# One-core two-block network in fp32 halves: the shifted norm ahead of the first FFN is shared out over three engines, and the later stages' tiles begin at other offsets

## What is computed

```python
x = x + gt1 * ((g_att * y_att + g_rwkv * y_rwkv) @ w_o[l])
h = rms_norm(x, norm2_w[l]) * (1.0 + sc2) + sh2
x = x + gt2 * conv_ffn(h, w_up[l], conv_w[l], conv_b[l], w_down[l])
```

## Time and profile before

| | |
|---|---|
| median of 3 runs | 2418.88 us (2418.67 to 2420.12) |
| the profiled execution: time, span | 2418.01 us, 2416.7 us |
| PE busy | 2328.0 us of the span |
| DVE, ACT, POOL busy | 1434.3, 691.2, 884.0 us |
| mean granted TensorE clock | 0.986 of full speed |

### The profile page before, as it was taken

One profiled execution on the slowest core, in us unless ns is written; L12 is line 12 of the kernel. 1 busy time (PEld: TensorE's weight loads), 2 busy tenths in 40 slices (PEclk: granted clock), 3 DMA queues, 4 the chain that ended last, 5 costly groups with the idle time before them and its releaser, 6 DMA issues.

```text
span 2416.7 us, 33857 instructions
## 1 busy us (share of the span) xinstructions
PE 2328.0 (96%) x14384; PEld 1836.3 (76%) x14384; DVE 1434.3 (59%) x1782; ACT 691.2 (29%) x864; POOL 884.0 (37%) x418
## 2 busy tenths in 40 slices
PE   6999999799999999799999999999999999999998
PEld 4776776577776787588888777888878888888887
DVE  5222323678877513767675588788843467888633
ACT  3122122443443423222222233322222333222212
POOL 4313221111111344444444444444444434444442
PEclk8999999899999999899999999999999999999999
DMA  6433332212122243233333223333332323333331
GB/s 238 133 105 102 113 94 77 57 47 52 46 48 48 64 143 93 60 101 100 97 112 89 79 83 104 96 96 96 103 105 84 102 79 87 96 97 99 114 91 54
DMA packets 412038, 222.56 MB, mean 92 GB/s; under 512 B 33823, under 2 KB 409458, under 8 KB 410610
## 3 DMA queue, kind: packets, MB, share of 16 engines
q1 hardware_dynamic: 383074, 206.14, 29.5%
q10 hardware_dynamic: 28816, 14.27, 2.2%
HBM read 214.61 MB, written 5.77 MB: 91 GB/s over the span
## 4 chain that ended last, share of the span: by engine, by line
PE 89%; DVE 6%; DMA 2%; ACT 1%; issue 1%; POOL 1%; SPq 1%; ACTq 0%; DVEq 0%; POOLq 0%
PE bank L312 88%; PE bank L315 1%; SPq L1514 0%; DMA rw_sixteen<-inverses 0%; DMA inverses<-rw_solved 0%; DVE h_low L2096 0%; DMA w_raw<-in_w_att_out 0%; DVE g_c L2302 0%; POOL w_low L308 0%; DVE sq L664 0%; DVE rw_keep L1480 0%; DVE sq L660 0%; DVE rw_terms L1566 0%; DMA vec_rows<-in_c 0%; DVE sq L566 0%
## 5 line engine op out<-in xcount | busy, mean ns | idle before, releaser
L308 POOL TENSOR_TENSOR w_low<-w_raw,w_high 128x1024 fp32r<-128x1024 f32 (+1 forms) x331 | 849.4, 2568 | 1462.2 <-ACT w_high L301 1462.2
L312 PE MATMUL bank<-h_high,w_high 128*128 128x512 f32 x2008 | 809.2, 403 | 25.8 <-DVE h_low L671 9.6
L312 PE MATMUL bank<-h_low,w_high 128*128 128x512 f32 x2008 | 787.5, 392 | 0.0
L301 ACT CAST w_high<-w_raw 128x1024 fp32r<-128x1024 f32 (+1 forms) x331 | 358.6, 1085 | 885.7 <-PE bank L312 863.5
L312 PE MATMUL bank<-h_high,w_low 128*128 128x512 f32 x2008 | 510.2, 393 | 0.0
L312 PEld LDWEIGHTS bank<-h_high,w_high 128*128 128x128 f32 x2008 | 379.1, 189 | 132.2 <-issue 27.1
L312 PEld LDWEIGHTS bank<-h_high,w_low 128*128 128x128 f32 x2008 | 376.0, 188 | 84.4 <-issue 5.3
L312 PEld LDWEIGHTS bank<-h_low,w_high 128*128 128x128 f32 x2008 | 379.9, 189 | 78.7 <-issue 4.1
L312 PE MATMUL bank<-g_high,w_high 128*128 128x512 f32 x352 | 139.1, 395 | 2.3 <-ACT g_c L2281 2.3
L312 PE MATMUL bank<-g_low,w_high 128*128 128x512 f32 x352 | 138.9, 395 | 0.0
L2174 DVE TENSOR_TENSOR x_res<-bank,x_res 128x512 f32<-128x512 f32 x32 | 22.1, 689 | 168.4 <-PE bank L312 168.3
(11 more groups left out here) (375 smaller groups left out, 2820.4 us busy)
## 6 DMA issues: line engine op xcount, KB each, us to landing
w_raw<-in_w_in SPq DMA_DIRECT2D x54, 512.0 KB, 4.9
w_raw<-in_w_up SPq DMA_DIRECT2D x44, 512.0 KB, 3.8
w_raw<-in_w_ffn_gate SPq DMA_DIRECT2D x44, 512.0 KB, 3.8
w_raw<-in_w_ffn_up SPq DMA_DIRECT2D x44, 512.0 KB, 3.9
w_raw<-in_w_ffn_down SPq DMA_DIRECT2D x32, 704.0 KB, 4.5
w_raw<-in_w_ada SPq DMA_DIRECT2D x32, 512.0 KB, 3.8
w_raw<-in_w_in ACTq DMA_DIRECT2D x25, 512.0 KB, 4.1
w_raw<-in_w_down SPq DMA_DIRECT2D x16, 704.0 KB, 4.5
```

Source lines behind the costliest of these rows:

```text
L301: self.A.copy(self.w_high[:, u % SPLIT_SLOTS, 0:k * P], self.raw_of(key)[:, 0:k * P]).then_inc(*self.S.rounded(*key))
L308: self.G.tensor_tensor(self.w_low[:, slot, 0:k * P], self.raw_of(key)[:, 0:k * P], self.w_high[:, slot, 0:k * P].bitcast(F32), ALU.subtrac ...
L312: return self.T.matmul(out, lhsT, rhs, start=start, stop=stop, skip_group_check=True)
```

## The change

It has two parts.

**The shifted norm** (`shifted_norm` in place of `norm`, `h_dve`, `h_act`, `h_pool`). The last square is no longer added by DVE: PE accumulates ones x rinv (the first seven squares), and then ones x sq (the eighth). The second unit of the FFN, ("f", 0, 1), is rounded by ACT and lowered by POOL ahead of the root. The engines then share the tiles. Even tiles: DVE makes sq = x * gain * rinv, ACT adds the shift while rounding into h_high, and DVE makes h_low = (sq + shift) - h_high. Odd tiles: POOL makes rooted = x * rinv, ACT makes h_high = rooted * gain + shift, then less = h_high - shift, and DVE makes h_low = rooted * gain - less. PE (`first_pair_pe`) runs four matmuls for each tile, two units at once, and both low passes behind them.

**The placement.** A tile of 32 bytes (`shift_less`) and one of 96 bytes (`lead`) come ahead of the large tiles, and one of 64 bytes (`lead_shared`) within the scope of the mixers. Nothing reads the last two. Start addresses, bytes over a multiple of 256:

| tiles | before | after |
|---|---|---|
| x_res, h_high, h_low, w_raw, w_high, w_low, rinv, sq | 128 | 128 |
| f_high, f_low, f_c, and the same of g0 and g1 | 0 | 128 |
| ev_high, ev_low, od_high, od_low | 0 | 128 |
| mg_a, mg_r (high and low), mg_both, att, mixed | 192 | 128 |
| the RWKV tiles rw_ar to rw_reach | 192 | 128 |
| ident, ones, head_ones | 160 | 192 |

```diff
--- before.py
+++ after.py
@@ -647,42 +647,6 @@
         for k in range(DT):
             V.scalar_tensor_tensor(src[:, k, :], src[:, k, :], gain(k), self.rinv[:], ALU.mult,
                                    ALU.mult).then_inc(*S_.dve_norm(name, "scaled", k))
-
-    def h_dve(self, name, src, gain, shift=None):
...
-    def h_low_of(self, queue, name, k):
...
-    def h_pool(self, name):
...
-    def h_act(self, name, shift=False):
...
-    def h_ready(self, name):
-        return lambda k: [(self.S.h_low_odd if k % 2 else self.S.h_low_even).at(name, k)]
@@ -2187,7 +2151,10 @@
                 V.wait_ge(*self.own("dve"))
                 V.tensor_scalar(x, x, first(n), None, ALU.mult).then_inc(*S_.dve_norm())
                 V.wait_ge(*self.own("dve"))
-            self.add_square(self.rinv, x, name, "squares", n)
+            if name == "wo" and n == DT - 1:
+                V.tensor_tensor(square, x, x, ALU.mult).then_inc(*S_.dve_norm(name, "squares", n))
+            else:
+                self.add_square(self.rinv, x, name, "squares", n)
             if gain and not to:
                 V.tensor_scalar(x, x, gain(n), None, ALU.mult).then_inc(*S_.residual("gained", n))
             if to and not first:
@@ -2222,14 +2189,64 @@
-    def norm(self, name, before, gain, shift=None):
-
-        self.sum_pe(name, self.S.dve_norm.at(before, "squares", DT - 1))
-        self.sum_dve(name)
-        self.root_act(name)
-        self.h_dve(name, self.x, gain, shift)
-        self.h_act(name, shift is not None)
-        self.h_pool(name)
+    def shifted_norm(self, before):
+        T, A, V, G, S_ = self.T, self.A, self.V, self.G, self.S
+        rooted, less = self.f_c[:, 0, 0, :], self.f_c[:, 1, 0, :]
+        gain, shift = self.gain2, lambda k: self.mod[:, 3 * DT + k:3 * DT + k + 1]
+        T.wait_ge(*S_.dve_norm.at(before, "squares", DT - 2))
+        self.empty(7)
+        self.mm(self.bank[7][:], self.ones[:], self.rinv[:], True, False)
+        T.wait_ge(*S_.dve_norm.at(before, "squares", DT - 1))
+        self.mm(self.bank[7][:], self.ones[:], self.sq[:, 0, :], False, True).then_inc(*S_.norm_sum("ffn"))
+        self.round_unit(("f", 0, 1))
+        self.root_act("ffn")
+        for k in range(DT):
+            if k % 2:
+                A.wait_ge(*S_.h_low_odd.at("ffn", k))
+                A.activation(self.h_high[:, k, :], rooted, ACT.Identity, bias=shift(k),
+                             scale=gain[:, k:k + 1]).then_inc(*S_.act_norm("ffn", "high", k))
+                if k > 2:
+                    A.wait_ge(*S_.h_low_even.at("ffn", k - 2))
+                A.wait_ge(*self.own("act"))
+                A.activation(less, self.h_high[:, k, :].bitcast(F32), ACT.Identity,
+                             bias=self.shift_less[:, k:k + 1]).then_inc(*S_.act_norm("ffn", "less", k))
+            else:
+                A.wait_ge(*S_.dve_norm.at("ffn", "normed", k))
+                A.activation(self.h_high[:, k, :], self.sq[:, k // 2 % 2, :], ACT.Identity,
+                             bias=shift(k)).then_inc(*S_.act_norm("ffn", "high", k))
+        V.tensor_scalar(self.shift_less[:], self.mod[:, 3 * DT:4 * DT], -1.0, None, ALU.mult).then_inc(*S_.dve_norm("ffn", "less"))
+        self.sum_dve("ffn")
+        V.wait_ge(*S_.act_norm.at("ffn", "root"))
+        def normed(k):
+            V.wait_ge(*self.own("dve"))
+            V.scalar_tensor_tensor(self.sq[:, k // 2 % 2, :], self.x[:, k, :], gain[:, k:k + 1], self.rinv[:], ALU.mult,
+                                   ALU.mult).then_inc(*S_.dve_norm("ffn", "normed", k))
+        normed(0)
+        for k in range(DT):
+            if k % 2 == 0 and k + 2 < DT:
+                normed(k + 2)
+            if k % 2:
+                V.wait_ge(*S_.act_norm.at("ffn", "less", k))
+                V.scalar_tensor_tensor(self.h_low[:, k, :], rooted, gain[:, k:k + 1], less, ALU.mult,
+                                       ALU.subtract).then_inc(*S_.h_low_even("ffn", k))
+            else:
+                V.wait_ge(*S_.act_norm.at("ffn", "high", k))
+                V.scalar_tensor_tensor(self.h_low[:, k, :], self.sq[:, k // 2 % 2, :], shift(k),
+                                       self.h_high[:, k, :].bitcast(F32), ALU.add, ALU.subtract).then_inc(*S_.h_low_even("ffn", k))
+        self.lower_unit(("f", 0, 1))
+        G.wait_ge(*S_.act_norm.at("ffn", "root"))
+        for k in range(1, DT, 2):
+            if k > 2:
+                G.wait_ge(*S_.h_low_even.at("ffn", k - 2))
+            G.tensor_tensor(rooted, self.x[:, k, :], self.rinv[:], ALU.mult).then_inc(*S_.h_low_odd("ffn", k))
@@ -2239,20 +2256,24 @@
             self.f_high = self.sb(f"{name}_high", [P, FT, S], F32R, ctx)
             self.f_low = self.sb(f"{name}_low", [P, FT, S], F32R, ctx)
             self.f_c = self.sb(f"{name}_c", [P, 2, 2, S], F32, ctx)
+            if not before:
+                self.shifted_norm("wo")
             self.ffn_pe(name, norm, both, before)
             self.ffn_act(name, norm, biases, before)
             if before:
                 self.ffn_ahead_dve(name, norm, taps)
             else:
                 self.ffn_dve(name, taps, biases, both)
-            self.ffn_pool(name)
+            self.ffn_pool(name, before)
             self.project(f"{name}_down", name, FT, scale, following, self.f_high, self.f_low,
                          lambda k: [self.S.parts.at(name, k)], **to)
     def ffn_pe(self, name, norm, both, before):
-        ready = self.ahead(norm) if before else self.h_ready(norm)
+        ready = self.ahead(norm) if before else None
+        if not before:
+            self.first_pair_pe(name, norm)
         for n in range(FT):
-            for j in range(2):
+            for j in range(2) if n or before else ():
                 b = 2 * (n % 2) + j
                 self.empty(b)
                 self.product((name, n, j), self.bank[b][:], *self.h_parts(), ready=ready)
@@ -2262,6 +2283,27 @@
                 ready = None
         self.end("pe", name)
+    def first_pair_pe(self, name, norm):
+        T, S_ = self.T, self.S
+        keys = [(name, 0, 0), (name, 0, 1)]
+        slots = [self.number[key] % SPLIT_SLOTS for key in keys]
+        tile = lambda t, j, k: t[:, slots[j], k * P:(k + 1) * P]
+        for j, key in enumerate(keys):
+            T.wait_ge(*S_.rounded.at(*key))
+            self.empty(j)
+        for k in range(DT):
+            T.wait_ge(*S_.h_low_even.at(norm, k))
+            for j in range(2):
+                self.mm(self.bank[j][:], tile(self.w_high, j, k), self.h_high[:, k, :], k == 0, False)
+                self.mm(self.bank[j][:], tile(self.w_high, j, k), self.h_low[:, k, :], False, False)
+        for j, key in enumerate(keys):
+            T.wait_ge(*S_.lowered.at(*key))
+            for k in range(DT):
+                ins = self.mm(self.bank[j][:], tile(self.w_low, j, k), self.h_high[:, k, :], False, k == DT - 1)
+            ins.then_inc(*S_.product(*key))
+            self.emptied[j] = (S_.conv, key)
     def ffn_act(self, name, norm, biases, before):
         A, S_ = self.A, self.S
         if not before:
@@ -2269,7 +2311,8 @@
         for n in range(FT):
             for j in range(2):
                 if j == 0:
-                    self.round_unit((name, n, 1))
+                    if n or before:
+                        self.round_unit((name, n, 1))
                 else:
                     self.round_unit((name, n + 1, 0) if n + 1 < FT else (f"{name}_down", 0, 0))
                     if before and n == 0:
@@ -2342,9 +2385,10 @@
                                     ALU.subtract).then_inc(*S_.parts(name, n))
         self.end("dve", name)
-    def ffn_pool(self, name):
+    def ffn_pool(self, name, before):
         for n in range(FT):
-            self.lower_unit((name, n, 1))
+            if n or before:
+                self.lower_unit((name, n, 1))
             self.lower_unit((name, n + 1, 0) if n + 1 < FT else (f"{name}_down", 0, 0))
         self.end("pool", name)
@@ -2792,6 +2836,7 @@
         self.sq = self.sb("sq", [P, 2, S])
         self.mod = self.sb("mod", [P, 6 * DT])
         self.rinv_first, self.gain_even = self.sb("rinv_first", [P, S]), self.sb("gain_even", [P, DT])
+        self.shift_less = self.sb("shift_less", [P, DT])
         self.gain1, self.gain2 = self.sb("gain1", [P, DT]), self.sb("gain2", [P, DT])
         self.ident = self.sb("ident", [P, P])
         self.ident_bf = self.sb("ident_bf", [P, P], BF16)
@@ -2806,10 +2851,13 @@
             for name, n in group:
                 self.where[name] = g * P + row
                 row += n
+        self.lead = self.sb("lead", [P, 24])
         self.plan()
         mod, col = self.mod, self.col
         shared = self.ctx.enter_context(ExitStack())
         self.rwkv_shared(shared)
+        self.lead_shared = self.sb("lead_shared", [P, 16], F32, shared)
         self.masks_room = self.sb("att_masks", [P, 2, S], F32, shared)
         with ExitStack() as scope:
```

(12 more changed lines are left out.)

## The result

The changed kernel takes 2402.89 us (median of 4 runs, 2402.19 to 2403.35) against 2419.25 us for the kernel before (2418.67 to 2420.12): a ratio of 0.9924, 95% interval 0.9912 to 0.9937. The forecast was 2401.2 us, the range 2397 to 2408. The profiled execution took 2403.35 us with a span of 2401.8 us.

The account below looks back on a forecast made before the run. PE bounds the kernel, busy 96% of the span. From 2418.01 us, 12.6 for the placement and 5.1 for the norm come off, giving 2400.3; the median lies 0.87 higher, so 2401.2 us, range 2397 to 2408.

Parts of the forecast that it names:

- The pitch goes with the streamed tile's offset: Dense PE streams: f, g0, g1, ev, od and mg tiles all reach h's 226.7 ns a matmul, 12.6 us in sum.
- The Trainium skill's 215.7 ns: Documented start distance of back-to-back 512-column matmuls on the full clock, no address named; by it the placement is worth nothing.
- The rival that would end there, 2413.8 us: Offset does not set the pitch (stage or SBUF region does); only the norm's 5.1 us counts; chance 0.09.
- The rival without a gain from the norm: Ring POOL, ACT, ACT, DVE longer than walked, clock stays low; only the placement counts, 2406.3 us; chance 0.11.
- The sum of squares gives 0.1 us: Before the norm's mean: PE's second product starts 0.74 us earlier, but shift_less waits for POOL, leaving 0.1 us.
- The tiles: Norm before the first FFN: new sharing takes 4.03 us a pair against 4.1, so the tiles themselves gain little.
- R: The end of the norm's root, 1006.52 in the profile before; times after it are counted from there.
- The walk: Step-by-step timing of DVE, POOL and ACT through the norm's new tile order, using prices from the old profile.
- PE gains through the second unit: First FFN: four matmuls a tile fill the waits; second unit ends at R + 21.0 against R + 26.0, gaining 5.0 us.
- The other rivals: RWKV stage's small matmuls pay for the moved tiles, slower than before, chance 0.03; neither part does anything, 2418.9 us, chance 0.03.
- the forecast's 17.7: Whole kernel: the predicted saving, 12.6 us from the placement and 5.1 us from the norm.

Follow-up runs that it names:

- the run with all at 0: The changed kernel with 128 bytes ahead of x_res, so x, h, weights and later stages' tiles begin at 0 over a multiple of 256; 2405.57 us.

## Why the prediction was right, point by point

- *The pitch goes with the streamed tile's offset.* Four of five sizes were right: f 3.5 (predicted 3.5), g0 and g1 6.0 (6.0), ev 1.2 (1.3), mg 0.8 (0.7). The fifth was not: od was put at 1.1 and came out at -0.5, its pitch outweighed by the fall of the clock, so the placement was 11.0 and not 12.6. The mechanism was only half right. The step "h begins at 128 bytes over a multiple of 256 and is the fastest" took the offset as absolute; what counts is that it equals the weights' offset. I had written that the weights lie at 128 in every case and drew nothing from it. For this change both readings give the same sum, so that the forecast held is luck in this respect: the absolute reading would have put the run with all at 0 some 42 us too high. The working also says that the DMA share of the slow windows was no higher than that of h; for mg it was 0.68 against 0.35. After the change mg's unit has 226.7 ns with a share of 0.70, so the load was not the cause.
- *The Trainium skill's 215.7 ns*, page "TensorE: Matmul & The Clock Gate", section "Wait — 56ns, not 53.3ns?": no stream here reached it. The trace of the changed kernel shows 226.67 ns in each dense stage, that of the kernel before up to 233.33 ns, at the same full clock. The rival that would end there, 2413.8 us, is out: the placement alone gave a ratio of 0.9953 and its f tiles 226.67 ns. The rival without a gain from the norm is out by the norm alone, 0.9967.
- *The sum of squares gives 0.1 us.* Small as said, and for the reason given: shift_less waited 2.31 us for POOL. Against the last `wo` matmuls the mean came 0.26 us earlier.
- *The tiles.* Predicted a pair in 4.03 us and the last tile at R + 16.1; measured 3.81 and 16.8. The walk let DVE take the port first. In fact POOL, whose row starts 0.05 us later (1007.30 against 1007.25), took 1.26 us, DVE's first tile took 1.85 and ended 0.55 after POOL, and ACT got it only at 1009.14. That put the first pair 0.85 us behind the walk. The next two pairs were 0.2 us shorter than walked and the last one 0.2 us longer.
- *PE gains through the second unit.* Predicted R + 21.0 and 5.0 us; measured R + 21.5 and 4.7 in all. The version with one unit at a time lost all of it and 1.4 us more (R + 27.4). The clock came back before the last tile, as the walk assumed.
- *The other rivals.* The RWKV stage did not pay: from its first solved block to the merge it was 376.8 us before and 376.2 after. Over all 14 profiles it was 375.0 to 380.4 us, the longest with the old placement, where the rival needs 17.7 us.
- *What was not foreseen*: two falls of the clock, 1.7 and 1.6 us. The one in od belongs to this placement, as every profile with it shows, and the one at `wo` to the execution. Together they take 3.3 us off the forecast's 17.7, and the last stage, which happened to be 1.1 us shorter, gives part of it back. The range had room for both.

## What to carry to other kernels

Where matmuls follow one another without a gap, divide a stage's length by its count, stage by stage; a few ns beside the same operation are worth a look, since over a whole kernel they add up: with the weights displaced this one took 34.6 us more. Then look at the clock of each stage too, since here od, with its faster stream, lost 1.6 us to it. Give the streamed tiles and the weight tiles the same start address modulo 256 bytes; a few unused bytes ahead of a tile do it. In a wait of PE that tiles release one by one, run two products a tile, and keep small operations with SBUF operands off the queue that makes the mean while GpSimd works (here the mean came 0.93 us earlier, which the whole time does not show).

## What the runs showed of the hardware

- The distance between starts of dense fp32r matmuls of 128 x 512 depends on (streamed tile's offset - weight tile's offset) modulo 256: 0 gives 226.67 ns, +64 gives 228.89 ns (three places in two kernels, and mg before), -64, -32, +32, +96 and 128 give 233.33 ns (at 128 also 232.4, in g0 and od of the kernel before), and -96 gives 234.3 ns. The differences of 0, +64, -64 and 128 were seen with weights at 128 and at 0, those of 32 and 96 only at 128. It holds for each matmul for itself: with w_low alone displaced only the passes with w_low slow down. Why the steps have these sizes, and why +64 and -64 differ, is open.
- A DVE operation of 128 x 8 elements took 2.31 us beside a lowering on POOL and ended 0.03 us after it. When both start together behind the root, DVE's 128 x 512 takes 1.85 to 1.88 us instead of 0.75 and ends 0.55 us after POOL's, though POOL's row starts 0.05 us later. So the order of such close rows is not the order in which they get the port.
- Behind waits of PE of 2.2 to 2.8 us the clock fell (for 3.41 us in the two windows above) in some profiles and not in others. Each fall cost 1.4 to 1.7 us. At the start of `wo` it came and stayed away in the same kernel; in od, behind 2.83 us each time, it came in all eight profiles with the streamed tile at the weights' offset, in one other, and in none of five. It hid the 0.93 us that shift_less gave back. What decides it was not tested.
